# Row rotations issued by SP, retention values centred before use, in-bank probabilities in a two-block transformer kernel

## The reference

```python
def group_norm(x, g):                       # on each retention head's output, 128 features
    mu = jnp.mean(xf, axis=-1, keepdims=True)
    xc = xf - mu
    return (xc * lax.rsqrt(jnp.mean(xc * xc, axis=-1, keepdims=True) + EPS)) * g

# retention: o_intra + o_cross, which is (decayed scores of q and k) @ v for every token
ro = group_norm(retention(rq, rk, rv), ret_norm)
ro = jax.nn.silu(rg) * ro

# differential attention, 4 heads, queries in 4 blocks of 128, m = 0, 1 the two sibling score maps
sc = jnp.einsum('bqhmd,bkhmd->bhmqk', q_blk, k) * scale - slopes * dist
p = jax.nn.softmax(jnp.where(dist >= 0, sc, NEG_BIG), axis=-1)
a = p[:, :, 0] - lam * p[:, :, 1]
return jnp.einsum('bhqk,bkhe->bqhe', a, v)

# mixer A: x * cos + rotated(x) * sin, rotated = rows of a head exchanged in groups of 32
```

## Time and profile before

| | before |
|---|---|
| median of 3 runs (lowest, highest) | 2110.91 us (2106.84, 2114.45) |
| the profiled execution: its time, its span | 2108.74 us, 2106.9 us |
| PE busy | 2054.5 us, 98% of the span |
| POOL, DVE, ACT busy | 1386.9, 750.0, 510.3 us |
| transfers | 195.26 MB, mean 93 GB/s |
| share of PE in the chain that ended last | 91% |

### The profile page before, as it was taken

How to read it: one execution, slowest core, us unless ns; L and a number is a source line. 1 busy time by engine, 2 the same in 40 slices (tenths; PEclk the granted TensorE clock), 3 DMA queues, 4 the chain that set the end, 5 groups by cost and what they waited for, 6 DMA issues and landing times.

```text
span 2106.9 us, 28827 instructions
## 1 busy us (share of the span) xinstructions
PE 2054.5 (98%) x9102; PEld 1642.8 (78%) x9102; DVE 750.0 (36%) x1214; ACT 510.3 (24%) x963; POOL 1386.9 (66%) x1372
## 2 busy tenths in 40 slices
PE   8999999999999999999999999999899999999997
PEld 6878676788888888878888887777677678888885
DVE  3135455343210221442240244355764552221024
ACT  2034333412200211331110021245643321110011
POOL 6654243477777777667777788655676367777675
PEclk9999999999999999999999999999999999999998
DMA  7321112132232233222333234222222122332231
GB/s 241 115 81 61 60 61 60 61 100 95 94 100 96 93 110 98 92 88 91 100 98 93 98 100 170 80 70 80 80 91 90 40 80 91 98 100 94 96 100 60
DMA packets 58470, 195.26 MB, mean 93 GB/s; under 512 B 7039, under 2 KB 9983, under 8 KB 58020
## 3 DMA queue, kind: packets, MB, share of 16 engines
q1 hardware_dynamic: 52364, 184.12, 26.9%
q10 hardware_dynamic: 6040, 10.24, 1.5%
HBM read 189.60 MB, written 4.21 MB: 92 GB/s over the span
## 4 chain that ended last, share of the span: by engine, by line
PE 91%; DVE 4%; ACT 2%; issue 2%; POOL 1%; ACTq 0%; DMA 0%; SPq 0%; DVEq 0%; POOLq 0%
PE acc L283 26%; PE acc L284 26%; PE acc L285 26%; PE st L329 2%; PE ob L770 1%; PE sc L754 1%; PE sc L1636 1%; PE acc L995 1%; PE acc L996 1%; PE acc L997 1%; PE tp L762 1%; DVE arena L1755 1%; ACTq L716 0%; DVE hr L360 0%; POOL w_hi L1847 0%
## 5 line engine op out<-in xcount | busy, mean ns | idle before, releaser
L1849 POOL TENSOR_TENSOR w_lo<-w_raw,w_hi 128x512 fp32r<-128x512 f32 x684 | 923.4, 1350 | 57.0
L1847 POOL TENSOR_SCALAR w_hi<-w_raw 128x512 fp32r<-128x512 f32 x684 | 465.8, 681 | 643.5 <-PE acc L285 597.8
L283 PE MATMUL acc<-h_hi,w_hi 128*128 128x512 f32 x1864 | 746.9, 401 | 13.9 <-DVE h_lo L1984 8.7
L285 PE MATMUL acc<-h_hi,w_lo 128*128 128x512 f32 x1864 | 727.9, 391 | 0.0
L284 PE MATMUL acc<-h_lo,w_hi 128*128 128x512 f32 x1864 | 727.4, 390 | 0.0
L283 PEld LDWEIGHTS acc<-h_hi,w_hi 128*128 128x128 f32 x1864 | 350.8, 188 | 100.6 <-issue 20.4
L284 PEld LDWEIGHTS acc<-h_lo,w_hi 128*128 128x128 f32 x1864 | 351.1, 188 | 78.3 <-issue 7.9
L285 PEld LDWEIGHTS acc<-h_hi,w_lo 128*128 128x128 f32 x1864 | 350.8, 188 | 74.0
L283 PE MATMUL acc<-hid_hi,w_hi 128*128 128x512 f32 x608 | 237.0, 390 | 0.7 <-POOL w_lo L1849 0.7
L285 PE MATMUL acc<-hid_hi,w_lo 128*128 128x512 f32 x608 | 236.7, 389 | 0.0
L284 PE MATMUL acc<-hid_lo,w_hi 128*128 128x512 f32 x608 | 236.7, 389 | 0.0
(11 more groups left out here) (286 smaller groups left out, 1856.0 us busy)
## 6 DMA issues: line engine op xcount, KB each, us to landing
w_raw<-in_wstream SPq DMA_DIRECT2D x341, 512.0 KB, 3.5
x<-in_xT SPq DMA_DIRECT2D x8, 256.0 KB, 6.4
bias_skew<-bias_rows ACTq DMA_DIRECT2D x8, 256.0 KB, 5.4
out_y<-x SPq DMA_DIRECT2D x8, 256.0 KB, 2.2
ssum<-arena ACTq DMA_DIRECT2D x20, 64.0 KB, 3.1
btmp<-arena ACTq DMA_DIRECT2D x20, 64.0 KB, 3.7
arena<-in_memT ACTq DMA_DIRECT2D x1, 1024.0 KB, 6.4
arena<-in_decay ACTq DMA_DIRECT2D x1, 1024.0 KB, 9.4
```

Of the source, the lines that this page charges most:

```text
L283: nc.tensor.matmul(dst, w_hi[:, slot, k, :], xh[:, k, :], start=first, stop=False)
L285: done = nc.tensor.matmul(dst, w_lo[:, slot, k, :], xh[:, k, :], start=False, stop=last)
L1847: nc.gpsimd.tensor_scalar(w_hi[:, slot, ks, :], w_raw[:, raw, ks, :], 1.0, 0.0, ALU.mult, ALU.add).then_inc(w_rounded, 1)
L1849: nc.gpsimd.tensor_tensor(w_lo[:, slot, ks, :], w_raw[:, raw, ks, :], w_hi[:, slot, ks, :].bitcast(F32), ALU.subtract).then_inc(w_split, 1)
```

## The change

1. The row exchanges leave ACT. SP issues them (`rope_rotate_sp`), each item's four transfers behind a certain weight transfer (`ROPE_LOAD`: the one seven units on), after waits for `acc_read` and for the DVE reader of two items before. The first 48 units of SP's loop are written out for it.
2. `b_add_dve(1)` stands ahead of `rope_scale_dve(4)` and `scaled1` of gate unit 1.
3. Retention values are centred when they are turned (`ret_v_dve`: a DVE sum and a DVE multiply-add per head in place of the ACT copy), since the mean over an output's features is linear in the values. The turns stand behind units 5, 7, 8 and 9 of `ret_proj`. The mean's matmul, and DVE's subtraction, are gone.
4. In differential attention p1 stays in PSUM: scores, bias, exponential of m = 1 are all in one bank, `sc[1]` or `tp[1]` in turn. `combine` reads it there. `turn` has only `tp[0]` left, so it waits for the copy of the tile before, and scores for m = 1 get two more waits: `d_a` and, for tile 1 on, `d_v` = 4, the ACT copy of the last head's turned values out of `tp[1]`.
5. From the norm `dq3` on, L353's result goes into the bank `st` in place of `vb`, so that the next `stat_pe` (and `pv` of the memory attention) waits for the Newton step instead.

```diff
@@ stat_pe, stat_v_dve, stat_newton_dve
-            pe.wait_ge(stat_v, q)
+            pe.wait_ge(*((stat_v, q) if q <= STAT["dq3"] else (stat_rstd, q)))
...
-            nc.vector.scalar_tensor_tensor(vb[:, 0:width], total[:, 0:width], n * eps, vb[:, 0:width], ALU.add, ALU.mult).then_inc(stat_v, 1)
+            to = vb if STAT[name] < STAT["dq3"] else st
+            nc.vector.scalar_tensor_tensor(to[:, 0:width], total[:, 0:width], n * eps, vb[:, 0:width], ALU.add, ALU.mult).then_inc(stat_v, 1)
...
-            nc.vector.scalar_tensor_tensor(dst, vb[:, 0:width], -3.0 * n, dst, ALU.add, ALU.mult).then_inc(stat_rstd, 1)
+            v = vb if STAT[name] < STAT["dq3"] else st
+            nc.vector.scalar_tensor_tensor(dst, v[:, 0:width], -3.0 * n, dst, ALU.add, ALU.mult).then_inc(stat_rstd, 1)
@@ rope_sq_act and the new rope_rotate_sp
-            act.wait_ge(s("a_rot_used"), counted(j - 1))
-            for q in range(4):
-                act.dma_start(rot[j % 2][32 * q:32 * q + 32, :], z_a(item(j))[32 * (q ^ 1):32 * (q ^ 1) + 32, :]).then_inc(s(f"a_rot{j % 2}"), 16)
+        ROPE_LOAD = {}
+        for _j in range(10):
+            _u = U0["a_proj"] + item(_j) if _j < 6 else U0["gates"] + 2 * (_j - 6)
+            ROPE_LOAD[_u + RAW + 1] = _j
+        def rope_rotate_sp(sp, j):
+            sp.wait_ge(acc_read, G0["a_proj"] + item(j) + 1)
+            sp.wait_ge(s("a_rot_used"), counted(j - 1))
+            for q in range(4):
+                sp.dma_start(rot[j % 2][32 * q:32 * q + 32, :], z_a(item(j))[32 * (q ^ 1):32 * (q ^ 1) + 32, :]).then_inc(s(f"a_rot{j % 2}"), 16)
@@ SP's program
-            with sp.Fori(1, UNITS // RAW) as i:
+            for u in range(RAW, 8 * RAW):
+                sp.wait_ge(w_split, 2 * u - 2 * RAW + 2)
+                sp.dma_start(w_raw[:, u % RAW], wstream[u]).then_inc(w_landed[u % RAW], 16)
+                if u in ROPE_LOAD:
+                    rope_rotate_sp(sp, ROPE_LOAD[u])
+            with sp.Fori(8, UNITS // RAW) as i:
@@ mixer_a_dve, in the loop over heads
                 norm(h, 3)
+                if h == 0:
+                    b_add_dve(dve, 1, ob[:])
                 if h + 4 < 10:
                     rope_scale_dve(dve, h + 4)
                 scaled1(dve, "gates", 2 * h + 1, gate_z(2 * h + 1))
-                if h == 0:
-                    b_add_dve(dve, 1, ob[:])
@@ retention_pe, retention_dve (retention_act loses its four copies)
-            pe.wait_ge(acc_read, G0["ret_proj"] + 4)
-            for h in range(4):
-                pe.wait_ge(s("r_v"), counted(h - 1))
-                for t in range(4):
-                    m = nc.tensor.transpose(tp[h % 2][:, t * P:(t + 1) * P], a2(dv0 + h)[:, t * P:(t + 1) * P], ident)
-                m.then_inc(s("r_vtr"), 1)
             pe.wait_ge(acc_read, G0["ret_proj"] + 12)
...
-                pe.wait_ge(s("r_o"), h + 1)
-                pe.wait_ge(s("r_xc"), h)
-                nc.tensor.matmul(tp[0], ones, tmp[:, 0, :], start=True, stop=True).then_inc(s("r_mu"), 1)
                 out1(pe, "diff_proj", 4 * h + 3, 1, h1_hi, h1_lo)
...
-                nc.vector.tensor_copy(tmp[:, 0, :], ob[:]).then_inc(s("r_o"), 1)
+                nc.vector.tensor_copy(tmp[:, 1, :], ob[:]).then_inc(s("r_xc"), 1)
...
-                dve.wait_ge(s("r_mu"), h + 1)
-                nc.vector.scalar_tensor_tensor(tmp[:, 1, :], tp[0], -1.0 / 128, tmp[:, 0, :], ALU.mult, ALU.add).then_inc(s("r_xc"), 1)
@@ ret_proj_pe, ret_proj_dve
             out_loop(pe, "ret_proj", 2, 6, h1_hi, h1_lo)
+            ret_v_turn_pe(pe, 0)
             out1(pe, "ret_proj", 6, 0, h1_hi, h1_lo)
             stat_pe(pe, "mem", [ssum[:, 0:MEM]], [(s("mem_sum"), KT + 1)], width=MEM)
-            out1(pe, "ret_proj", 7, 1, h1_hi, h1_lo)
-            out_loop(pe, "ret_proj", 8, 12, h1_hi, h1_lo)
+            for u in range(7, 12):
+                out1(pe, "ret_proj", u, u % 2, h1_hi, h1_lo)
+                if u < 10:
+                    ret_v_turn_pe(pe, u - 6)
...
+        def ret_v_dve(dve, h):
+            v = tp[h % 2].rearrange("p (t c) -> p t c", t=QT)
+            total = nmax[:, 4 * (h % 2):4 * (h % 2) + 4]
+            dve.wait_ge(s("r_vtr"), h + 1)
+            nc.vector.tensor_reduce(total, v, AX.X, ALU.add).then_inc(s("r_vm"), 1)
+            dve.wait_ge(s("r_vm"), h + 1)
+            nc.vector.scalar_tensor_tensor(a2(rv0 + h).rearrange("p (t c) -> p t c", t=QT), total.unsqueeze(2).to_broadcast([P, QT, P]),
+                                           -1.0 / 128, v, ALU.mult, ALU.add).then_inc(s("r_v"), 1)
...
                 scaled1(dve, "ret_proj", u, a2(dv0 + u) if u < 4 else a2(u - 4))
+                if 6 <= u <= 9:
+                    ret_v_dve(dve, u - 6)
@@ diff: p_d, scores, turn, and pv of the memory attention
-        p_d = [[a2(28), a2(29)], [a2(32), a2(31)]]
+        p_d = [[a2(28), a2(29)], [sc[1], tp[1]]]
+        def d_score_to(qt, m):
+            return p_d[1][qt % 2] if m else sc[0]
...
+                if m:
+                    pe.wait_ge(s("d_a"), counted(4 * h + qt - 1))
+                    pe.wait_ge(s("d_v"), 4 if (h, qt) > (0, 0) else 0)
...
-                pe.wait_ge(turned_copy, TILES0["diff"] + e - 1)
+                pe.wait_ge(turned_copy, TILES0["diff"] + e)
...
-                    pe.wait_ge(stat_v, STAT[f"mq{h + 1}"] + 1)
+                    pe.wait_ge(stat_rstd, STAT[f"mq{h + 1}"] + 1)
```

More of the change, by code:

```diff
@@ L1183, in d_scored_dve @@
             dve.wait_ge(s("d_a"), counted(4 * h + qt - 1))
[L1184 removed]
+            nc.vector.tensor_tensor_reduce(p_d[m][(e // 2) % 2][:, 0:w], d_score_to(qt, m)[:, 0:w], alibi_s[:, h, SEQ - w:SEQ], 1.0,
                                            -LOWEST, ALU.add, ALU.min, mx[:, e % 8:e % 8 + 1]).then_inc(row_max, 1)
         def retention_pe(pe):
[L1188 to L1193 removed]
             pe.wait_ge(acc_read, G0["ret_proj"] + 12)
@@ L1212, in retention_pe @@
                 pe.wait_ge(s("r_v"), 4)
-                pe.wait_ge(s("r_o"), h)
+                pe.wait_ge(s("r_xc"), h)
                 for kt in range(QT):
@@ L1240, in retention_act @@
         def retention_act(act):
-            for h in range(4):
-                act.wait_ge(s("r_vtr"), h + 1)
-                nc.scalar.copy(a2(rv0 + h), tp[h % 2]).then_inc(s("r_v"), 1)
             def dsq(j):
@@ L1341, in ret_proj_pe, with ret_v_turn_pe @@
             out_loop(pe, "ret_proj", 2, 6, h1_hi, h1_lo)
+            ret_v_turn_pe(pe, 0)
             out1(pe, "ret_proj", 6, 0, h1_hi, h1_lo)
             stat_pe(pe, "mem", [ssum[:, 0:MEM]], [(s("mem_sum"), KT + 1)], width=MEM)
-            out1(pe, "ret_proj", 7, 1, h1_hi, h1_lo)
-            out_loop(pe, "ret_proj", 8, 12, h1_hi, h1_lo)
+            for u in range(7, 12):
+                out1(pe, "ret_proj", u, u % 2, h1_hi, h1_lo)
+                if u < 10:
+                    ret_v_turn_pe(pe, u - 6)
+        def ret_v_turn_pe(pe, h):
+            pe.wait_ge(acc_read, G0["ret_proj"] + 4)
+            pe.wait_ge(s("r_v"), counted(h - 1))
+            for t in range(4):
+                m = nc.tensor.transpose(tp[h % 2][:, t * P:(t + 1) * P], a2(dv0 + h)[:, t * P:(t + 1) * P], ident)
+            m.then_inc(s("r_vtr"), 1)
+        def ret_v_dve(dve, h):
[6 more added lines that the diff above has]
+                                           -1.0 / 128, v, ALU.mult, ALU.add).then_inc(s("r_v"), 1)
         def ret_proj_dve(dve):
@@ L1412, in score @@
                 pe.wait_ge(s("d_qk"), 2 * h + 2)
-                nc.tensor.matmul(sc[m][:, 0:(qt + 1) * P], a2(dq0 + h)[64 * m:64 * m + 64, qt * P:(qt + 1) * P],
+                if m:
+                    pe.wait_ge(s("d_a"), counted(4 * h + qt - 1))
+                    pe.wait_ge(s("d_v"), 4 if (h, qt) > (0, 0) else 0)
+                nc.tensor.matmul(d_score_to(qt, m)[:, 0:(qt + 1) * P], a2(dq0 + h)[64 * m:64 * m + 64, qt * P:(qt + 1) * P],
                                  a2(dk0 + h)[64 * m:64 * m + 64, 0:(qt + 1) * P], start=True, stop=True).then_inc(scores, 1)
@@ L1418, in turn @@
                 pe.wait_ge(s("d_a"), e + 1)
-                pe.wait_ge(turned_copy, TILES0["diff"] + e - 1)
+                pe.wait_ge(turned_copy, TILES0["diff"] + e)
                 pe.wait_ge(s("d_v"), 4)
                 for kt in range(qt + 1):
-                    m = nc.tensor.transpose(tp[e % 2][:, kt * P:(kt + 1) * P], p_d[0][e % 2][:, kt * P:(kt + 1) * P], ident)
+                    m = nc.tensor.transpose(tp[0][:, kt * P:(kt + 1) * P], p_d[0][e % 2][:, kt * P:(kt + 1) * P], ident)
                 m.then_inc(turned, 1)
@@ L1468, in copy_pt @@
                 nc.scalar.copy(pt_2[:, 0:qt + 1, qt * P:(qt + 1) * P],
-                               tp[e % 2][:, 0:(qt + 1) * P].rearrange("p (t c) -> p t c", c=P)).then_inc(turned_copy, 1)
+                               tp[0][:, 0:(qt + 1) * P].rearrange("p (t c) -> p t c", c=P)).then_inc(turned_copy, 1)
             def o_copy(h):
```

1 line of the change is left out of this document (removed).

## The result

| | before | after |
|---|---|---|
| median of 5 runs each (lowest, highest), us | 2109.10 (2106.84, 2114.45) | 2095.04 (2094.07, 2097.07) |
| profiled execution: span, us | 2106.9 | 2095.3 |
| ratio of after to before | | 0.9933, 95% interval 0.9917 to 0.9948 |

The change makes the kernel 14.1 us faster. 1.8 of the 6.8 us between forecast and result are the yardstick (the median of before is 2109.1 over five runs, 2110.9 over the three that were shown); the other 5.0 are the gain.

What follows compares the result with a forecast made beforehand. PE was taken as the bound, busy 2054.5 of 2106.9 us. Terms 4.9 + 1.5 + 3.4 - 0.4 - 0.8 + 0.5 = 9.1 us, off the shown median 2110.91, gave 2101.8 us; range 2095.5 to 2107.5.

Steps and rivals of the forecast that it cites:

- the 4.9 us of the rotary exchanges: Rotary items and mixer B's end: without ACT's issues, waits of 2.8 and 2.1 us go, 4.9 us gained.
- the 0.5 us for the rest of differential attention: Differential attention after its start: 0.5 us gained from shorter Newton steps and last tiles, bounds 0 and 3.9.
- the start of differential attention: Tile 1's second score waits for ACT's copy out of tp[1]; the wait moves forward, net cost 0.8 us.
- rival 2: Rotary exchanges: another wait replaces the removed ones, the 4.9 us gain is lost, time 2106.7; chance 0.16.
- a wait can't be shorter than nothing: Rotary exchanges: the reason given for 4.9 us as the upper bound of the gain.
- The addition: Mixer A, head 0: addition put first, so `pv` loses its 1.5 us wait; bounds 1.0 and 1.5.
- The matmuls: Retention: four matmuls with ones go, 0.86 us each, 3.4 us gained in full.
- The start was forecast at -0.4: Retention's first score: starts 1.31 us earlier, but 1.74 us of transposes stand between units; cost 0.4 us.
- the unbroken ACT chain: Differential attention, tiles 3 and 4: ACT works without a break, so an earlier turn makes PE wait longer for the square.
- shorter Newton steps: Differential attention: named with last tiles as the source of the 0.5 us gain.
- The risk: Tile 3: waiting on the Newton step instead of L353 can cost PE 0.7 us, hidden there by ACT's chain.
- Rival 1: Differential attention: waits for `combine` close too, 3.9 us in place of 0.5; 2098.4, or 2096 with key squares; chance 0.15.

Runs made afterwards that it cites:

- b_order: Kernel before, with ACT's two copies at mixer B's last step moved ahead of the exchange issues and item 4's square; 2103.79 us against 2107.76, ratio 0.9981.
- b_diff: Kernel before with parts 4 and 5 of the change alone; 2106.66 us against 2108.53, ratio 0.9989.
- b_ret: Kernel before with part 3 of the change alone (retention values centred when turned); one run, 2107.46 us.
- b_sp: Kernel before with part 1 of the change alone (SP issues the exchanges); 2101.68 us against 2107.76, ratio 0.9970.
- a_tp0: Changed kernel with the last head's values turned through bank tp[0] instead of tp[1]; 2093.24 us against 2107.76 for before, ratio 0.9932.
- best: The changed kernel with last head's values turned through tp[0], plus memory-key norms spread over later tiles; 2091.52 us against 2106.63 for before, ratio 0.9929.
- best_again: The version `best` run again, on the chip of the changed kernel's second runs; 2091.57 us against 2108.53 for before, ratio 0.9919.
- after_again: The changed kernel, unaltered, profiled a second time; tile 1's first score to tile 0's turn took 6.68 us, against 9.41 in the first profile.
- the second set: The changed kernel's second set of runs, on one chip with `best_again`; 2094.66 us against 2108.53 for before, ratio 0.9934.

## Why the prediction was wrong

Two terms of the sum failed: the 4.9 us of the rotary exchanges, with the bound put on them, which came out as 8.4 where half clock stood behind the wait, and the 0.5 us for the rest of differential attention, which came out as 3.3. A third, the start of differential attention, left the clock out as well.

**Rotary exchanges.** The mechanism held: 2.9 us for the items, 2.2 for mixer B's wait, SP without cost, and rival 2 did not come. The step that failed is "a wait can't be shorter than nothing", which made 4.9 the upper bound. A wait can cost more than its length. `b_order` shows it with one moved copy: 5.5 us for a wait of 2.09, against the profile of before, in which half clock stood behind it; in `b_diff`, where none did, the same wait cost 3.3 us less.

**The addition** was right (1.5 alone, 1.7 in the changed kernel).

**Retention.** The matmuls were right to 0.1 us. The start was forecast at -0.4 and took -0.6 from the first turn to the first score, in the changed kernel, in `b_ret` and in each other profile with part 3; I had let the score start 0.06 us behind DVE's read. The rest of the step of -1.4 is gone ahead of the first turn, at the unit that waits for GpSimd (0.84 here, 0.71 in before, 0.03 in `b_sp`, `b_order` and `a_tp0`) and at the units behind it. Over the nine profiles with part 3 this stretch gives anything from -0.9 to +0.35, over the four others 0 to +0.3. No instruction of part 3 stands in it, and profiles of one and the same kernel differ by 0.9 there (`best` and `best_again`, +0.1 and -0.8), so it moves from trace to trace by itself.

**Start of differential attention.** "The wait moves forward and costs 0.8 us more than it saves" was right in the waits: 0.9 in `after_again`, where the clock stayed full (6.68 against 5.77 us). It left out the 2.7 us of half clock in the profiled execution. `a_tp0` removes both.

**Differential attention, the rest.** "I give this part 0.5 us" is the term of the sum that was mis-sized; it measured 2.4, with 0.85 more in memory attention. The argument from the unbroken ACT chain was right for what it was about: with `combine` in PSUM alone the waits fell by 0.1 us (8.5 to 8.4). Part 5, which I had named with its "shorter Newton steps" inside the 0.5 and priced otherwise only as a risk, closed 1.4 us of them and the 0.9 us of memory attention. The risk was there too, 1.10 us in place of 0.36 at tile 3. Of the 2.4 us the waits explain 1.5; the other 0.9 is PE busy time (76.4 against 75.5 us). It comes with parts 4 and 5, since `b_diff` has the same 75.5; its cause was not tried.

**The sum** without the clock is 9.1 + 0.1 (items) + 0.1 (mixer B) + 0.2 (addition) - 1.0 (retention's start and GpSimd) - 0.1 (start of differential attention) + 1.9 + 0.85 = 11.15, and with 3.3 - 2.7 for the clock 11.75, against the 11.65 of the two traces. The medians differ by 14.1, and by 13.9 in the second set. The 2.4 us between lie in which executions were profiled: that of after was the slowest of its five, 2097.07, 2.0 above the median, and that of before 0.4 below its own. Rival 1 named the right place (the waits for `combine` close too), and its 2098.4, or 2096, is nearest to the result; its cause, the shorter `combine`, was not the one.

## What to carry to other kernels

In a kernel whose PE never rests, look at the granted clock behind each of PE's waits before pricing it: a wait of 2 us was worth 5.5 where half clock stood behind it, and one of 0.9 just its 0.9. A term that is bounded by "the wait can't be shorter than nothing" needs that column beside it, and so does each wait that a change adds. Where an edit moves one input of a DVE operation from SBUF to PSUM while GpSimd works, look at what stands behind it too: the Newton step stayed at 0.69 us here, and the pair of products behind it fell from 2.67 to 2.45.
